# Routing of a mixture of experts rebuilt: transposes and logits inside the last projection, bf16 ranks, three blocks looked up

## The chip, the cores and the metric

The kernel runs on one core of a Trainium2 chip. The metric is the device time of one execution in microseconds (us); lower is better.

## The reference

One decoder block over 512 tokens of 1024 features. A token mixer (short gated convolution and dilated windowed attention, merged by sigmoid gates, then the projection `w_out`) is added to x; then comes the mixture of experts:

```python
h = rms_norm(x, norm2_g)
logits = h @ w_router + b_router                     # 512 x 32
top_vals, top_idx = lax.top_k(logits, 4)
gates = softmax(top_vals)
# each (token, expert) pair gets a place; an expert's places are padded to blocks of 128
# for each block, with its expert e:
gu = xb @ w_gate_up[e] + b_gate_up[e]                # 128 x 2048
act = (clip(up, -7, 7) + 1) * (min(gate, 7) * sigmoid(1.702 * min(gate, 7)))
y = act @ w_down[e] + b_down[e]
out[token] += y * gate_of_the_pair
```

## The kernel before

The engines run programs of their own, tied together by semaphores: PE (matmul), ACT, DVE, POOL, and SP, which issues loads. Large products split each fp32 operand into a high and a low part and take three matmuls (`three`, lines 574 to 576); ACT makes the high part of a weight chunk, DVE the low one (`split`, `split_expert`, lines 865, 987, 1085, 1236). A weight chunk is 1 MB; six buffers take them in, and one is asked for again when DVE is through with it.

**The front** is a fixed list of steps (`STEPS`). Its last four chunks are the projection (`wo`), in units of half the contraction: unit `UF - 1` is the last. Each chunk covers 256 columns, and DVE adds its four blocks of 128 tokens to `x2` (line 1153), while ACT squares and sums them (line 915).

**The routing** then runs as one chain. PE turns `x2` (32 transposes, line 712); ACT and DVE copy the eight results with the gain of the norm; PE makes 32 x 512 logits in eight matmuls (line 721); ACT copies them and PE turns them back. DVE divides by the norm and adds the bias (line 1265), finds maxima and indices (1269, 1270), makes one-hot rows (1273) and their sum (1279). PE sums ranks (729, 733) and counts. For the first two experts' blocks DVE marks which token has which rank (1326), PE multiplies that by token numbers (742), and DVE writes the indices (1338); POOL gathers the rows of block 0 (1473) out of `expert_inputs`, a copy of the normed rows in DRAM which DVE made (1259) and SP stored. PE turns them (754), ACT and DVE split them (1009, 1358), and the expert blocks begin. DVE's first weight split, `split_expert(0, 0)`, stands between the normed rows and line 1265.

**All other blocks** are looked up in a table. DVE works out a place for each of the 16 x 128 pairs, POOL writes them as 16 indirect DMAs (line 1487), reads the table back (1491), stores `x2` as the initial output in five DMAs of 512 KB (1551, 1552), and from then on copies one column per block (1527) and gathers by it (1473). So the first block that hangs on the table is block 2.

**A block** is 16 steps of gate and up (first a bias matmul, line 778), eight of down. The rows of the next block are turned after the second and fourth of the down steps; in block 0, which has no down step, at the end. There the down biases of all experts are also added to `x2`: PE makes each half in eight matmuls (808), DVE adds it in two operations (1397), and block 1 waits for all four:

```python
pe.wait_ge(x2_biased, 2)
down_bias(1)
pe.wait_ge(x2_biased, 4)
```

## Time and profile before

| | |
|---|---|
| Time, three runs | 1715.55 us median (1714.28 to 1716.5) |
| The profiled execution | 1712.57 us, span 1710.7 |
| Busy: PE, DVE, ACT, POOL | 1652.5, 1351.3, 1095.7, 318.4 us |
| Chain that ended last | PE 91%, DVE, POOL and DMA 2% each |
| Mean granted clock of PE | 0.987 |

The span runs from the first to the last instruction. The busy time of PE is modelled, and pipelined matmuls overlap, so the distance from one start to the next tells more than a duration. In a row, the bracket at the end gives how long the engine was idle before it and what ended that.

### The profile page before, as it was taken

How to read it: one execution, taken by the hardware profiler on the slowest of the kernel's cores; microseconds unless marked ns; L12 is line 12 of the kernel's file. 1: busy time of each engine (PE TensorE's matmuls, PEld its weight loads, DVE VectorE, ACT ScalarE, POOL GpSimd, SP SyncE). 2: the span in 40 equal slices, each digit the busy share in tenths (PEclk: the TensorE clock that was granted, in tenths of full speed). 3: DMA queues.
4: the chain of work that ended last, by engine and by line, in shares of the span. 5: the costliest groups of instructions: out<-in, count | busy, mean ns of one | idle time of the engine just before them, and what ended most of it. 6: DMA issues, size and time to landing. Idle time of an engine off the chain costs nothing.

```text
span 1710.7 us, 23870 instructions
## 1 busy us (share of the span) xinstructions
PE 1652.5 (97%) x7974; PEld 1349.4 (79%) x7974; DVE 1351.3 (79%) x1091; ACT 1095.7 (64%) x989; POOL 318.4 (19%) x174
## 2 busy tenths in 40 slices
PE   7999999999997899999999999999999999999995
PEld 5788777888885678888888888888888888888884
DVE  3874555543537989899998999989999899998994
ACT  4324333422344567787777877778777787777873
POOL 0000000510002741221112221132111221113210
PEclk9999999999997999999999999999999999999998
DMA  8222222332436899999999999999999999999993
GB/s 267 79 75 74 74 75 75 93 102 95 143 144 210 296 368 378 367 374 377 383 378 369 366 381 384 376 365 373 383 377 378 366 371 384 382 376 365 376 384 95
DMA packets 211683, 482.34 MB, mean 282 GB/s; under 512 B 12539, under 2 KB 55075, under 8 KB 195123
## 3 DMA queue, kind: packets, MB, share of 16 engines
q1 hardware_dynamic: 201024, 453.99, 70.6%
q0 software_dynamic: 10624, 27.87, 7.9%
q8 instruction: 24, 0.39, 0.1%
q14 instruction: 11, 0.09, 0.0%
HBM read 469.05 MB, written 21.67 MB: 287 GB/s over the span
## 4 chain that ended last, share of the span: by engine, by line
PE 91%; DVE 2%; POOL 2%; DMA 2%; issue 2%; ACT 1%; SPq 0%; POOLq 0%; ACTq 0%; DVEq 0%
PE ps L574 28%; PE ps L576 27%; PE ps L575 27%; PE ps L754 2%; PE ps L760 2%; PE ps L778 2%; POOL slot_records L1487 1%; DMA r<-expert_inputs,uix 1%; PE ps L688 1%; PE ps L677 1%; PE ps L649 1%; PE ps L668 0%; PE ps L721 0%; PE ps L594 0%; ACT work L967 0%
## 5 line engine op out<-in xcount | busy, mean ns | idle before, releaser
L1236 DVE TENSOR_TENSOR zT<-raw,zT 128x2048 fp32r<-128x2048 f32 x96 | 220.0, 2293 | 57.4 <-ACT zT L987 54.6
L1236 DVE TENSOR_TENSOR w_lo<-more_raw,w_hi 128x2048 fp32r<-128x2048 f32 x96 | 217.3, 2290 | 17.7 <-ACT w_hi L987 17.7
L1236 DVE TENSOR_TENSOR zT<-more_raw,zT 128x2048 fp32r<-128x2048 f32 x96 | 219.8, 2290 | 0.0
L1236 DVE TENSOR_TENSOR w_lo<-raw,w_hi 128x2048 fp32r<-128x2048 f32 x96 | 217.1, 2289 | 0.9 <-ACT w_hi L987 0.9
L574 PE MATMUL ps<-w_hi,xT 128*128 128x512 f32 x512 | 216.6, 423 | 0.0
L574 PE MATMUL ps<-zT,xT 128*128 128x512 f32 x512 | 202.4, 395 | 0.0
L576 PE MATMUL ps<-w_hi,xT 128*128 128x512 f32 x512 | 200.7, 392 | 0.0
L575 PE MATMUL ps<-w_lo,xT 128*128 128x512 f32 x512 | 200.7, 392 | 0.0
L987 ACT ACTIVATE zT<-more_raw 128x2048 fp32r<-128x2048 f32 x96 | 183.5, 1911 | 25.6 <-PE ps L576 25.6
L576 PE MATMUL ps<-zT,xT 128*128 128x512 f32 x512 | 199.5, 390 | 0.0
L575 PE MATMUL ps<-zT,xT 128*128 128x512 f32 x512 | 199.3, 389 | 0.0
L987 ACT ACTIVATE w_hi<-raw 128x2048 fp32r<-128x2048 f32 x96 | 183.4, 1910 | 21.3 <-PE ps L576 21.3
L1540 POOL DMA_INDIRECT out<-r,uix x32 | 51.3, 1603 | 714.3 <-ACT r L1036 707.9
L987 ACT ACTIVATE zT<-raw 128x2048 fp32r<-128x2048 f32 x96 | 183.3, 1911 | 0.0
L1085 DVE TENSOR_TENSOR w_lo<-raw,w_hi 128x1024 fp32r<-128x1024 f32 x76 | 101.6, 1349 | 102.5 <-ACT w_hi L865 102.4
L987 ACT ACTIVATE w_hi<-more_raw 128x2048 fp32r<-128x2048 f32 x96 | 180.0, 1909 | 0.0
L574 PE MATMUL ps<-hT,w_hi 128*128 128x512 f32 x416 | 167.3, 402 | 0.0
L575 PE MATMUL ps<-hT,w_hi 128*128 128x512 f32 x416 | 162.4, 390 | 0.0
L576 PE MATMUL ps<-hT,w_lo 128*128 128x512 f32 x416 | 162.0, 389 | 0.0
L865 ACT ACTIVATE w_hi<-raw 128x1024 fp32r<-128x1024 f32 x76 | 79.8, 1056 | 72.3 <-PE ps L576 70.8
L574 PEld LDWEIGHTS ps<-w_hi,xT 128*128 128x128 f32 x512 | 97.5, 190 | 25.2 <-issue 0.6
L576 PEld LDWEIGHTS ps<-w_hi,xT 128*128 128x128 f32 x512 | 96.8, 189 | 21.3
(240 smaller groups left out, 3356.9 us busy)
## 6 DMA issues: line engine op xcount, KB each, us to landing
more_raw<-in_w_gate_up SPq DMA_DIRECT2D x129, 1024.0 KB, 7.4
raw<-in_w_gate_up SPq DMA_DIRECT2D x127, 1024.0 KB, 7.0
raw<-in_w_down SPq DMA_DIRECT2D x65, 1024.0 KB, 8.0
more_raw<-in_w_down SPq DMA_DIRECT2D x63, 1024.0 KB, 7.2
raw<-in_w_in SPq DMA_DIRECT2D x29, 1024.0 KB, 5.2
r<-in_x SPq DMA_DIRECT2D x8, 512.0 KB, 7.1
raw<-in_w_branch_conv SPq DMA_DIRECT2D x4, 1024.0 KB, 4.7
raw<-in_w_out SPq DMA_DIRECT2D x4, 1024.0 KB, 4.7
```

The lines of the kernel that those rows point to most:

```text
L574: pe.matmul(dst, a_hi, b_hi, start=start, stop=False)
L575: pe.matmul(dst, a_hi, b_lo, start=False, stop=False)
L576: return pe.matmul(dst, a_lo, b_hi, start=False, stop=stop)
L649: pe.matmul(ps[:, EVENTS[ev][2], :], cst[:, C_BLK:C_BLK + P], yv[:, j % 2, :], start=True, stop=True).then_inc(done, 1)
L754: last = pe.transpose(ps[:, bk_T + half, P * k:P * k + P], xs[:, 4 * half + k::KD], ident)
L760: last = pe.transpose(ps[:, bk_T + half, P * k:P * k + P], act[:, half, k::4], ident)
L778: pe.matmul(ps[:, base + s, :], sel[:, bass.ds(g, 1), :], bpart[:, D * s + 512 * half:D * s + 512 * half + 512], start=True, stop=False)
L865: nc.scalar.activation(packed(w_hi, n), raw_unit(n, (n // 2) % RAW), ACT.Copy).then_inc(split_hi, 1)
L987: nc.scalar.activation(expert_pair(0, c), chunk, ACT.Copy).then_inc(split_hi, 2)
L1085: nc.vector.tensor_tensor(packed(w_lo, n), raw_unit(n, (n // 2) % RAW), packed(w_hi, n).bitcast(F32), ALU.subtract).then_inc(split_lo, 1)
L1236: nc.vector.tensor_tensor(expert_pair(1, c), chunk, expert_pair(0, c).bitcast(F32), ALU.subtract).then_inc(split_lo, 2)
L1540: nc.gpsimd.indirect_dma_start(out=out, out_offset=bass.IndirectOffsetOnAxis(ap=uix[:, 1:2], axis=0), in_=ysb, in_offset=None, compute_op= ...
```

## The change

- The gain is multiplied in on DVE behind each eviction of the projection, into `h2`. PE turns `h2` instead of `x2`: 16 transposes ahead of the last unit, 8 in its middle, the last 8 behind it. The copies to `h2T` are spread over ACT and DVE (`turn_copy`).
- The logits are made per block of 128 tokens, each in a column group of 32 of its own: four matmuls of 128 columns for each k. Four k are done inside the last unit. They are copied once as 128 x 128 and turned by one transpose.
- The norm's factor is applied to `h2` in place, two blocks on DVE, two on ACT; SP waits for each block by itself.
- DVE's routing works on all four blocks at once, with fewer waits between operations; the sum of one-hot rows is two additions instead of a reduction. Masks, triangle, ones, one-hot rows and token numbers are bf16 (a token number in two parts).
- Three blocks are looked up early: block 0's index first and alone, then 1 and 2. `split_expert(0, 0)` moves behind them. POOL gathers block 2's rows by `gather(4)`, behind the stores but without the table.
- `add_down_bias(1)` comes before `clamp_up(0, 1)`, and PE waits for three of the four additions.

The diff, cut to its core (removed lines of the routing can be seen above; the context is shortened):

```diff
 UPE = 2 * CPE
+GBANK = (0, 1, 2, 3, 0, 1, 3, 0)
 PAIRS = HPG // 2 * NB
...
         load_expert(0, c, 0, first=True)
-    sp.wait_ge(h2_ok, NB)
     for b in range(NB):
+        sp.wait_ge(h2_d if b < 2 else h2_a, b % 2 + 1)
         sp.dma_start(h2_v[:, b, :], h2[:, b, :]).then_inc(h2_out, 16)
...
             src = hT if name == "v" else zT
-            for b in range(NB):
+            for b in rows:
                 ev = EV[(name, 4 * i + b)]
...
                                  wh[:, k, :], wl[:, k, :], kk == 0, kk == KD - 1)
+                if n == UF - 1 and b < NB - 1:
+                    last.then_inc(last_rows, 1)
             return last
...
     for kind, n in STEPS:
-        if kind == "unit":
...
+    def turn_gained(k, rows):
+        pe.wait_ge(gained_ok, NB * (k // 2) + rows[-1] + 1)
+        for b in rows:
+            last = pe.transpose(ps[:, 4 + GBANK[k], P * b:P * b + P], h2[:, b, P * k:P * k + P], ident)
+        return last
+    def logits(k):
+        pe.wait_ge(h2T_d if k % 2 else h2T_a, k // 2 + 1)
         for b in range(NB):
...
+            last = pe.matmul(ps[NE * b:NE * b + NE, 6, 0:P], wr_sb[:, k, :], h2T[:, k, P * b:P * b + P],
+                             start=(k == 0), stop=(k == KD - 1))
+        return last
+    pe.wait_ge(freed["dve"], FREED[EV[("wo", 3 * NB - 1)]][1])
+    for k in range(4):
+        turn_gained(k, range(NB)).then_inc(h2T_pe, 1)
+    unit(UF - 1, rows=(0, 1))
+    pe.wait_ge(h2T_a, 1)
+    pe.wait_ge(h2T_d, 1)
+    for k in (4, 5):
+        turn_gained(k, range(NB)).then_inc(h2T_pe, 1)
     pe.wait_ge(wr_in, 32)
...
+    pe.wait_ge(h2T_a, 2)
+    for k in range(4):
+        logits(k)
+    unit(UF - 1, rows=(2, 3)).then_inc(used, 1)
+    for k in (4, 5):
+        logits(k)
+    for k in (6, 7):
+        turn_gained(k, range(3))
+    for k in (6, 7):
+        turn_gained(k, (3,)).then_inc(h2T_pe, 1)
+    logits(6)
+    logits(7).then_inc(logitsT_pe, 1)
     pe.wait_ge(logitsT_ok, 1)
...
+    pe.transpose(ps[:, 1, 0:P], lgT, ident).then_inc(logit_rows_pe, 1)
+    pe.wait_ge(const_h, 3)
     pe.wait_ge(chosen_ok, 1)
...
+    pe.matmul(ps[:, 1, 0:P], tri_h, mskh.rearrange("p b e -> p (b e)"), start=True, stop=False)
     for c in range(NB - 1):
...
+        last = pe.matmul(ps[:, 1, NE * (c + 1):P].rearrange("p (b e) -> p b e", b=later), ones_h,
+                         mskh[:, c:c + 1, :].to_broadcast([P, later, NE]), start=False, stop=(c == NB - 2))
     last.then_inc(ranks_pe, 1)
...
+        last = pe.matmul(ps[0:NE, 2, 0:1], mskh[:, b, :], ones_h[:, 0:1], start=(b == 0), stop=(b == NB - 1))
     last.then_inc(ranks_pe, 1)
...
+    def early_rows(e):
         pe.wait_ge(hot_ok, e + 1)
...
+            last = pe.matmul(ps[:, bk_T, 2 * e:2 * e + 2], hot[:, e, b, :], tok_h[:, b, :],
                              start=(b == 0), stop=(b == NB - 1))
...
+        return last
+    early_rows(0).then_inc(turned_pe, 1)
+    pe.wait_ge(turned_read, 1)
+    for e in range(1, EARLY):
+        last = early_rows(e)
+    last.then_inc(early_pe, 1)
     pe.wait_ge(blocks_ok, 1)
...
         last.then_inc(turned_pe, 1)
+    pe.wait_ge(early_ok, 1)
     pe.wait_ge(xs_in, 16)
...
     down_bias(1)
-    pe.wait_ge(x2_biased, 4)
+    pe.wait_ge(x2_biased, 3)
     with pe.Fori(1, nblk) as g:
...
         nc.scalar.activation(packed(w_hi, n), raw_unit(n, (n // 2) % RAW), ACT.Copy).then_inc(split_hi, 1)
+    def turn_copy(k):
+        sc.wait_ge(h2T_pe, k + 1)
+        nc.scalar.activation(h2T[:, k, :], ps[:, 4 + GBANK[k], :], ACT.Copy).then_inc(h2T_a, 1)
     sc.wait_ge(eps_ok, 1)
...
                         sc.wait_ge(merged_lo, KD)
+                        sc.wait_ge(logits_ok, PAIRS)
+                    if i == 3 and b == 0:
+                        turn_copy(0)
+                        turn_copy(2)
+                    if i == 3 and b == 2:
+                        turn_copy(4)
                     sc.wait_ge(freed["dve"], FREED[EV[("wo", NB * i + b)]][1])
...
                         sc.wait_ge(ssq, NB + NB * i + b)
-                    nc.scalar.activation(work[:, 0:256], x2[:, b, 256 * i:256 * i + 256], ACT.Square,
+                    nc.scalar.activation(squares, x2[:, b, 256 * i:256 * i + 256], ACT.Square,
                                          accum_out=stat[:, 32 + NB * b + i:33 + NB * b + i]).then_inc(ssq, 1)
...
                          bias=stat[:, 31:32]).then_inc(rstd_s, 1)
-    for k in range(0, KD, 2):
-        sc.wait_ge(h2T_pe, k + 1)
-        nc.scalar.activation(h2T[:, k, :], ps[:, k, :], ACT.Copy,
-                             scale=small[:, 34 + k:35 + k]).then_inc(h2T_a, 1)
+    turn_copy(6)
+    def scale_rows(b):
+        nc.scalar.activation(h2[:, b, :], h2[:, b, :], ACT.Copy, scale=stat[:, 16 + b:17 + b]).then_inc(h2_a, 1)
+    sc.wait_ge(rstd2_ok, 1)
+    sc.wait_ge(h2T_pe, KD)
+    scale_rows(2)
+    sc.wait_ge(logitsT_pe, 1)
+    sc.wait_ge(bias_parts_ok, 1)
+    nc.scalar.activation(lgT, ps[:, 6, 0:P], ACT.Copy).then_inc(logitsT_ok, 1)
+    scale_rows(3)
     for c in range(3):
         split_expert(0, c)
-    sc.wait_ge(logitsT_pe, 1)
-    sc.wait_ge(bias_parts_ok, 1)
-    nc.scalar.activation(lgT, ps[0:NE, 0, :], ACT.Copy).then_inc(logitsT_ok, 1)
     sc.wait_ge(top4_ok, 1)
...
                                        ALU.subtract).then_inc(freed["dve"], 1)
+    def turn_copy(k):
+        ve.wait_ge(h2T_pe, k + 1)
+        nc.vector.tensor_copy(h2T[:, k, :], ps[:, 4 + GBANK[k], :]).then_inc(h2T_d, 1)
     def convolve(m, t):
...
                 continue
+            if name == "wo" and i == 0:
+                ve.wait_ge(scores_pe, PAIRS)
+                nc.vector.tensor_copy(tri_h, cst[:, C_TRI:C_TRI + P]).then_inc(const_h, 1)
+                nc.vector.tensor_copy(ones_h, ones).then_inc(const_h, 1)
+                nc.vector.tensor_copy(mconst[:, 2 * P:2 * P + 2 * NB],
+                                      cst[:, C_TOK:C_TOK + 2 * NB]).then_inc(const_h, 1)
             if name in ("v", "wo"):
...
                     ev = EV[(name, NB * i + b)]
-                    ve.wait_ge(used, n + 1)
+                    if n == UF - 1 and b == 0:
+                        turn_copy(1)
+                        turn_copy(3)
+                    if n == UF - 1 and b == 2:
+                        turn_copy(5)
+                    if n == UF - 1 and b < NB - 1:
+                        ve.wait_ge(last_rows, b + 1)
+                    else:
+                        ve.wait_ge(used, n + 1)
                     src = ps[:, EVENTS[ev][2], 0:256]
...
                         nc.vector.tensor_tensor(dst, src, dst, ALU.add).then_inc(freed["dve"], 1)
+                        ve.wait_ge(freed["dve"], FREED[ev][1])
+                        if i == 0 and b == 0:
+                            ve.wait_ge(g2_in, 16)
+                        nc.vector.tensor_tensor(h2[:, b, 256 * i:256 * i + 256], dst,
+                                                g2b[:, 256 * i:256 * i + 256], ALU.mult).then_inc(gained_ok, 1)
                 continue
...
+    turn_copy(7)
     ve.wait_ge(rstd_s, 2)
...
     ve.wait_ge(rstd2_ok, 1)
+    ve.wait_ge(h2T_pe, KD)
+    for b in range(2):
+        nc.vector.tensor_scalar(h2[:, b, :], h2[:, b, :], stat[:, 16 + b:17 + b], None,
+                                ALU.mult).then_inc(h2_d, 1)
+    ve.wait_ge(logit_rows_pe, 1)
+    link(nc.vector.tensor_tensor(lgt, ps[:, 1, 0:P].rearrange("p (b e) -> p b e", b=NB),
+                                 stat[:, 16:20].unsqueeze(2).to_broadcast([P, NB, NE]), ALU.mult))
+    link(nc.vector.tensor_tensor(lgt, lgt, br_sb.unsqueeze(1).to_broadcast([P, NB, NE]), ALU.add))
     for b in range(NB):
...
+        last = nc.vector.max(top8[:, b, :], lgt[:, b, :])
     link(last)
...
+        last = nc.vector.max_index(idx8[:, b, :], top8[:, b, :], lgt[:, b, :])
+    link(last)
+    link(nc.vector.tensor_scalar(idxf, idx8[:, :, 0:TOPK], 1.0, None, ALU.add))
+    link(nc.vector.tensor_tensor(oh, idxf.rearrange("p b k -> p (b k)").unsqueeze(2).to_broadcast([P, NREC, NE]),
+                                 cst[:, C_IOTA:C_IOTA + NE].unsqueeze(1).to_broadcast([P, NREC, NE]),
+                                 ALU.is_equal))
+    link(nc.vector.tensor_tensor(msk2, ohk[:, :, 0:2], ohk[:, :, 2:4], ALU.add))
+    nc.vector.tensor_tensor(mskh, msk2[:, :, 0], msk2[:, :, 1], ALU.add).then_inc(chosen_ok, 1)
     nc.vector.tensor_tensor(gate, top8[:, :, 0:TOPK], top8[:, :, 0:1].to_broadcast([P, NB, TOPK]),
...
+    link(nc.vector.scalar_tensor_tensor(sg1, ps[:, 1, 0:P].rearrange("p (b e) -> p b e", b=NB), 1.0, mskh,
                                         ALU.add, ALU.mult))
...
+    def find(e):
         nc.vector.tensor_tensor(hot[:, e], cst[:, C_IOTA:C_IOTA + P].unsqueeze(1).to_broadcast([P, NB, P]),
...
                                 ALU.is_equal).then_inc(hot_ok, 1)
+    find(0)
     ve.wait_ge(ranks_pe, 2)
...
     link(nc.vector.tensor_scalar(nbk[:, 1:2], ps[0:NE, 2, 0:1], 2 * P + 0.5, None, ALU.is_gt))
+    ve.wait_ge(turned_pe, 1)
+    ve.wait_ge(ix_set, 1)
+    nc.vector.tensor_copy(stat[:, 26:27], ps[:, bk_T, 0:1]).then_inc(early_hi, 1)
+    ve.wait_ge(early_hi, 1)
+    nc.vector.scalar_tensor_tensor(uix[:, 0:1], stat[:, 26:27], float(OUT_OF_RANGE), ps[:, bk_T, 1:2],
+                                   ALU.add, ALU.add).then_inc(turned_read, 1)
+    for e in range(1, EARLY):
+        find(e)
     link(nc.vector.tensor_scalar(nbk[:, 2:3], ps[0:NE, 2, 0:1], 3 * P + 0.5, None, ALU.is_gt))
...
+    ve.wait_ge(early_pe, 1)
+    nc.vector.tensor_copy(stat[:, 27:29], ps[:, bk_T, 2:2 * EARLY:2]).then_inc(early_hi, 1)
+    ve.wait_ge(early_hi, 2)
+    nc.vector.scalar_tensor_tensor(uix[:, 3:5], stat[:, 27:29], float(OUT_OF_RANGE),
+                                   ps[:, bk_T, 3:2 * EARLY:2], ALU.add, ALU.add).then_inc(early_ok, 1)
+    split_expert(0, 0)
     for b in range(NB):
...
     turned(0, ROWS1, xTh[:, 4:8, :], xTl[:, 4:8, :], bk_T + 1)
+    add_down_bias(1)
     clamp_up(0, 1)
     activate(0, 1)
-    add_down_bias(1)
     split_expert(1, 1)
...
     gp.wait_ge(turned_pe, FIRST_ROWS)
+    gp.wait_ge(early_ok, 1)
     gather(3)
...
     gp.dma_start(out[S:S + P, :], x2[:, 0, :]).then_inc(out_set, 16)
+    gp.wait_ge(turned_pe, tile(1, BEGIN))
+    gather(4)
     gp.wait_ge(slots_in, 16)
-    gather_next(1)
     over_experts()
...
```

## Rows read from the trace of the kernel before

**Rows 1.** Windows: width, busy PE PEld DVE ACT POOL, PEclk, DMA share, GB/s.

```profile
518.00:520.00 2.00, 0.00 (x0) 0.00 (x0) 1.93 (x7) 0.86 (x2) 0.00 (x0) 0.56 0.86 234
...
800.00:1600.00 800.00, 800.00 (x3685) 654.91 (x3684) 744.14 (x495) 636.53 (x495) 173.76 (x90) 1.00 1.03 376
```

**Rows 2.** Timeline of PE: start, us, line, form, count [idle before <-releaser].

```profile
264.15 1.09 PE L688 MATMUL ps<-r 128*64 128x128 f32 x16
...
501.29 0.28 PE L575 MATMUL ps<-w_lo,zT 128*128 128x256 f32 x1
...
501.41 0.28 PE L576 MATMUL ps<-w_hi,zT 128*128 128x256 f32 x1
...
503.20 3.71 PE L712 MATMUL ps<-cst,r 128*128 128x128 f32 x32 [1.51 <-DVE r L1153]
...
506.85 7.05 PE L721 MATMUL ps<-work,r 128*32 128x512 f32 x16
...
520.25 0.79 PE L729 MATMUL ps<-r,cst 128*128 128x128 f32 x2 [5.24 <-DVE r L1279]
...
523.27 3.58 PE L742 MATMUL ps<-cst,work 128*128 128x1 f32 x16 [0.59 <-DVE work L1326]
...
535.74 1.04 PE L778 MATMUL ps<-r 96*128 96x512 bf16 x2 [1.42 <-DVE xT L1358]
...
568.80 1.03 PE L778 MATMUL ps<-r 96*128 96x512 bf16 x2 [4.71 <-DVE r L1397]
...
601.01 1.12 PE L754 MATMUL ps<-cst,r 128*128 128x128 f32 x4 [2.97 <-DMA r<-expert_inputs,uix]
...
612.96 0.61 PE L778 MATMUL ps<-r 96*128 96x512 bf16 x2
```

**Rows 3.** Timeline of DVE, same columns.

```profile
501.73 1.42 DVE L1153 TENSOR_TENSOR r<-ps,r 128x256 f32<-128x256 f32 x4 [10.10 <-PE ps L576]
...
515.05 0.72 DVE L1265 SCALAR_TENSOR_TENSOR r<-ps,stat,r 128x32 f32<-128x32 f32 x4 [0.35 <-PE ps L725]
...
517.91 0.17 DVE L1271 TENSOR_SCALAR r<-r 128x16 f32<-128x16 uint32 x1
...
519.14 1.05 DVE L1279 TENSOR_REDUCE r<-r 128x128 f32<-128x512 f32 x1
...
522.52 1.29 DVE L1326 TENSOR_TENSOR work<-cst,r 128x512 f32<-128x512 f32 x2
...
528.66 2.29 DVE L1236 TENSOR_TENSOR w_lo<-more_raw,w_hi 128x2048 fp32r<-128x2048 f32 x1
...
534.14 0.69 DVE L1358 TENSOR_TENSOR xT<-ps,xT 128x512 fp32r<-128x512 f32 x1 [2.73 <-ACT xT L1009]
...
566.00 2.35 DVE L1397 TENSOR_TENSOR r<-r,ps 128x1024 f32<-128x1024 f32 x2
```

**Rows 4.** Timeline of POOL, and its records as a group (busy, mean ns | idle before).

```profile
527.93 1.26 POOL L1473 DMA_INDIRECT r<-expert_inputs,uix  x1 [6.75 <-DVE uix L1338]
...
545.37 1.01 POOL L1487 DMA_INDIRECT slot_records<-rec,record_at  x1 [9.75 <-issue]
...
585.12 1.92 POOL L1527 COPY uix<-slots 128x1 uint32<-128x1 uint32 x1
...
587.87 2.90 POOL L1473 DMA_INDIRECT r<-expert_inputs,uix  x1 [0.83 <-POOL uix L1527]
...
L1487 POOL DMA_INDIRECT slot_records<-rec,record_at x16 | 24.9, 1558 | 14.3 <-issue 14.3
```

**Rows 5.** DMA issues in 584.58:584.7 and 587.5:588.5: count, KB each, us to landing.

```profile
out<-r POOLq DMA_DIRECT2D x2, 512.0 KB, 13.7
...
r<-expert_inputs,uix POOLq DMA_INDIRECT x1, 13.1
```

**Rows 6.** Groups by form: busy us, mean ns of one | idle before.

```profile
L1273 DVE TENSOR_TENSOR r<-r,cst 128x128 f32<-128x128 f32 x4 | 0.9, 287 | 0.0
...
L865 ACT ACTIVATE w_hi<-raw 128x1024 fp32r<-128x1024 f32 x76 | 79.8, 1056 | 72.3 <-PE ps L576 70.8 <-DMA raw<-in_w_in 1.6
```

More of the change, by code:

```diff
@@ L595, in _, with unit @@
                 last.then_inc(done, 1)
-            def unit(n, tiles=(0, 1)):
+            def unit(n, tiles=(0, 1), rows=range(NB)):
                 name, i = CHUNKS[n // 2]
@@ L693, in _ @@
             for kind, n in STEPS:
-                if kind == "unit":
+                if kind == "unit" and n < UF - 1:
                     unit(n, (1,) if ("half", n) in STEPS else (0, 1)).then_inc(used, 1)
@@ L705, in _ @@
                     values(n)
-            pe.wait_ge(freed["dve"], FREED[EV[("wo", 4 * NB - 1)]][1])
-            for k in range(KD):
-                for b in range(NB):
-                    last = pe.transpose(ps[:, k, P * b:P * b + P], x2[:, b, P * k:P * k + P], ident)
-                last.then_inc(h2T_pe, 1)
-            pe.wait_ge(wr_in, 32)
-            for k in range(KD):
-                if k == 0:
-                    pe.wait_ge(h2T_a, 1)
-                    pe.wait_ge(h2T_d, 1)
-                else:
-                    pe.wait_ge(h2T_d if k % 2 else h2T_a, k // 2 + 1)
-                last = pe.matmul(ps[0:NE, 0, :], wr_sb[:, k, :], h2T[:, k, :], start=(k == 0), stop=(k == KD - 1))
@@ L723, in _ @@
+            for k in (4, 5):
[6 more added lines that the diff above has]
+            logits(7).then_inc(logitsT_pe, 1)
             pe.wait_ge(logitsT_ok, 1)
-            for b in range(NB):
-                last = pe.transpose(ps[:, 1, NE * b:NE * b + NE], lgT[:, P * b:P * b + P], ident[0:NE, 0:NE])
-            last.then_inc(logit_rows_pe, 1)
+            pe.transpose(ps[:, 1, 0:P], lgT, ident).then_inc(logit_rows_pe, 1)
@@ L728, in _ @@
+            pe.wait_ge(const_h, 3)
             pe.wait_ge(chosen_ok, 1)
-            pe.matmul(ps[:, 1, 0:P], cst[:, C_TRI:C_TRI + P], msk.rearrange("p b e -> p (b e)"),
-                      start=True, stop=False)
+            pe.matmul(ps[:, 1, 0:P], tri_h, mskh.rearrange("p b e -> p (b e)"), start=True, stop=False)
             for c in range(NB - 1):
                 later = NB - 1 - c
-                last = pe.matmul(ps[:, 1, NE * (c + 1):P].rearrange("p (b e) -> p b e", b=later), ones,
-                                 msk[:, c:c + 1, :].to_broadcast([P, later, NE]), start=False, stop=(c == NB - 2))
+                last = pe.matmul(ps[:, 1, NE * (c + 1):P].rearrange("p (b e) -> p b e", b=later), ones_h,
+                                 mskh[:, c:c + 1, :].to_broadcast([P, later, NE]), start=False, stop=(c == NB - 2))
@@ L735, in _ @@
             last.then_inc(ranks_pe, 1)
             for b in range(NB):
-                last = pe.matmul(ps[0:NE, 2, 0:1], msk[:, b, :], ones[:, 0:1], start=(b == 0), stop=(b == NB - 1))
+                last = pe.matmul(ps[0:NE, 2, 0:1], mskh[:, b, :], ones_h[:, 0:1], start=(b == 0), stop=(b == NB - 1))
             last.then_inc(ranks_pe, 1)
-            for e in range(2):
+            def early_rows(e):
                 pe.wait_ge(hot_ok, e + 1)
                 for b in range(NB):
-                    last = pe.matmul(ps[:, bk_T, e:e + 1], hot[:, e, b, :], cst[:, C_TOK + b:C_TOK + b + 1],
+                    last = pe.matmul(ps[:, bk_T, 2 * e:2 * e + 2], hot[:, e, b, :], tok_h[:, b, :],
@@ L1256, in _ @@
-            ve.wait_ge(g2_in, 16)
             ve.wait_ge(rstd2_ok, 1)
-            for b in range(NB):
-                nc.vector.scalar_tensor_tensor(h2[:, b, :], x2[:, b, :], stat[:, 16 + b:17 + b], g2b,
-                                               ALU.mult, ALU.mult).then_inc(h2_ok, 1)
-            split_expert(0, 0)
-            ve.wait_ge(logit_rows_pe, 1)
-            for b in range(NB):
-                last = nc.vector.scalar_tensor_tensor(lgt[:, b, :], ps[:, 1, NE * b:NE * b + NE],
-                                                      stat[:, 16 + b:17 + b], br_sb, ALU.mult, ALU.add)
+            ve.wait_ge(h2T_pe, KD)
```

55 lines of the change are left out of this document (20 added, 35 removed).

## Prediction

> **What bounds the kernel now.** I first read the time by stretches. From 800 to 1600 us the matmul engine (PE) is busy all the time at the full clock [rows 1]: the expert blocks run at PE's pace, and what is gained ahead of them reaches the end one for one, as long as weights keep coming. So only the passage from the last projection matmul to block 2 matters. I then walked along it, engine by engine, in the timelines.
>
> PE finishes the projection, and DVE starts the last four evictions at 501.73. Then come, each waiting for the one before, 32 transposes, the logits (7.05), four small transposes, DVE's routing from 515.05 to 520.19 (519.14 + 1.05), the rank sums, the one-hot rows and their eight small products (3.58), the gather of block 0's rows and block 0 at 535.74 [rows 2, 3]. Block 1 starts at 568.80 after 4.71 us in which PE waited for the down-bias additions [rows 2, 3].
>
> There is a second chain, and it decides. POOL writes the 16 records from 545.37 on, loads the slots, sends out five 512 KB blocks, copies the column and gathers block 2's rows at 587.87 [rows 4]. This gather takes 13.1 us [rows 5]. PE has waited 2.97 for it when it goes on at 601.01, and block 2 starts at 612.96 [rows 2].
>
> **Up to the logits.** Sixteen transposes (columns 0 to 511) move ahead of the last unit, eight more into its middle; the work is the same, 3.71/32 = 0.116 each [rows 2]. What goes is the wait for four evictions plus squares and copies behind them. The price of 32 logit matmuls of 128 columns in four column groups isn't in the trace. Bounds: at the old pace of 7.05 us for 8 x 512 columns, 0.88 for each k, nothing is saved; wholly side by side, 0.22. The nearest row is the attention's product with values, two column groups of 64: 16 instructions, so 8 matmuls of 128 columns, took 1.09 where the pace of the logits (7.05/32 = 0.22 for 128 columns) gives 1.76 [rows 2]. They overlap, and an instruction comes about every 0.06. Eight instructions for a k then make 0.46, which I take.
>
> Timeline, on the clock of the trace. The last unit is 48 matmuls, 0.12 from one to the next (501.29 to 501.41), so 5.76, and its predecessor ends at 501.53 - 5.76 = 495.77 [rows 2]. Then 16 transposes 1.84, half of the unit 2.88, 8 transposes 0.93, four k of logits 1.84, the other half 2.88: the last row block is issued at 506.1. DVE evicts it from 506.3 (one of the four in 1.42, alone 0.42) and multiplies by the gain (the same size, 0.42 and a semaphore): 507.2 [rows 3]. Meanwhile PE does k 4 and 5 and six transposes. The last two transposes end at 508.1, the two copies out of PSUM (0.7 like any 128x512 operation of DVE) at 508.8, k 6 and 7 at 509.9. On ACT the scaling of 1024 columns (1.06 [rows 6]) stands ahead of the copy of the logits: 509.1 to 510.15, the copy some 0.3, one transpose: DVE starts the routing at 510.8 instead of 515.05. Gain 4.25; bounds 0.9 (0.88 for each k, three groups of which lie on the path) and 5.1 (0.22).
>
> At one place a rule speaks against this. The Trainium skill, "TensorEngine Tiling (Array Packing)", section Key Properties, says that a change of the tiling mode drains the array; the change has three more such switches than before. By it each switch would add a stop to PE's order where the trace's rows let me price none; no run here shows it for 32-column groups.
>
> **Up to the gather.** DVE's 5.14 us of routing fall: the four maxima and searches (515.8 to 517.91, 2.1) lose most of their eight waits, about 1.5 [rows 3]; four comparisons of 128 columns (0.287 alone [rows 6]) become one of 512 (0.7, no gain but one start); the reduction of 1.05 becomes additions of 256 and 128 columns, 0.42 + 0.29. With the two first operations (0.6) and the cast (0.2) about 3.8: gain 1.35. The rank sums run in fp32, two instructions each, from 520.25 until DVE reads them at 522.2, one operation of 0.3 ahead of the 522.52 of the one-hot rows [rows 2, 3]; in bf16 it is one instruction each, 0.22 at the pace of the sixteen in 3.58, so 0.8 to 0.9: gain 1.15 (bounds 0, if the two passes had overlapped, and 1.6). The first one-hot operation costs what it did. The products of 3.58 become four instructions instead of 16, at most 0.9 and, without fp32 loads, I take 0.55; DVE's reading becomes two operations instead of one (+0.2). From PE's 523.27 to POOL's 527.93 [rows 2, 4] were 4.66, I take 1.85: gain 2.8. Sum: 4.25 + 1.35 + 1.15 + 2.8 = 9.55, gather at 518.4. The rows must be in DRAM by then: ACT scales the last block until 511.6, its store takes 4 to 6, POOL's clearing 1: 517 to 518.5, just hidden, so a gain beyond this would stop here.
>
> **Block 0 starts with less.** Two more lookups (0.65 each), three small operations, the second index pair with its wait (0.7) and above all the weight split of 2.29, which before lay in PE's logits, now stand in DVE's queue behind the first index [rows 3]. Before, DVE had 2.73 us to spare in the gather's shadow, as the row of 534.14 shows. The new work is about 4.5. So DVE becomes the last one by 1.8, and block 0 starts 9.55 - 1.8 = **7.8** earlier, at 527.9. The sixth weight chunk is asked for only after this split, but it is used 16 us into the block: hidden.
>
> **Block 1.** The first half of the second bias addition (one of the two in 2.35) now comes before three operations of 0.7 and its other half: PE's 4.71 fall by about 3.0 [rows 2, 3]. The wait that is left, 1.7, is like the 1.51 after which the logits ran at full speed; 4.71 was followed by matmuls at 1.2 GHz (two bf16 ones of 512 columns in 1.03), as in 518 to 520, where the granted clock shows 0.56 after PE had stood since 515 [rows 1, 2]. So the clock's loss of 1.9 goes too (nine matmuls 0.2 longer). These 4.9 us bring PE only earlier to the gather of block 2. The second split of block 1 is late by 1 to 2 us now, inside the same shadow.
>
> **The gather of block 2.** Records, slots and stores follow DVE's places, so they move by 7.8. The copy (1.92) and its wait (0.83) ahead of the gather go, so it is issued 10.3 earlier. But the last two of the five stores needed 13.7 us [rows 5] and so landed near 598, the gather 3 us behind at 601: it is the queue behind which it stands, not the issue, that sets the landing. Only the stores' shift counts, 7.8, and about 1 more, since PE stands from about 586 and its weight buffers fill: less traffic beside the queue. PE goes on 8.8 earlier, from 601.0 to 592.2, again in the slow clock, and the 11.95 to block 2 stay. From there nothing differs. **Sum: 8.8.** Bounds of this term: 7.8 (nothing but the shift) and 10.3 (issue decides).
>
> The profiled execution took 1712.57 (span 1710.7, 1.9 around it); minus 8.8 is 1703.8. The median of the runs is 3.0 above that execution, so **1706.8**.
>
> **The rivals.**
> - The landing follows the issue, or the front gains its upper bounds: 10.3 to 12, about 1704.5. For it: the gather was 3 us behind the stores, so some of its time was its own. Chance 0.14.
> - The column groups don't overlap in fp32: 0.88 for each k, 3.4 more on the path, gain 5.3, time 1710.2. For it: no 32-column case in the trace; against it: the 64-column row. Chance 0.12.
> - The change does hardly anything: block 0 starts earlier, but DVE's queue, now with the split in front, and POOL's records eat it; gain under 3.4. That takes another 5 us in DVE's queue. Chance 0.07.
> - Slower: the records. They took 1.56 on average, 0.3 between, 0.97 to 2.88 each [rows 4], and short ones are those that meet a gap of DVE. With DVE packed tightly, all at the long form of 2.88 + 0.3, sixteen take 51 instead of 29.5: 21 later, minus 8.8, slower by 12, about 1728. It decides from a mean of 2.4 a record on. Against it: DVE was already busy nine tenths there. Chance 0.05. The Trainium skill, "SBUF — State Buffer", section "SBUF: two separate sides", gives a reason: GpSimd is blocked by whichever DVE operation holds the pair; by that page two-input DVE operations hinder only its reads, which would make this rival less likely.
>
> **The numbers.** My forecast, 7 to 10.3 less: 0.62. The range must hold 8 in 10: from 1703 (a gain of 12.5) to 1711.3 (4.3), which takes in the fp32 rival. A change within 0.2%, 3.4 us, is about what a measurement of this kernel can't tell from none. Faster: 0.62 + 0.14 + 0.12 = 0.88; within 0.2%: 0.07; slower 0.05.
>
> **What would show it.** The logits' 32 matmuls at 0.4 to 0.5 for four; routing on DVE starting near 510.8; the first gather near 518.4; block 0 near 528, released by DVE; no slow clock in block 1; PE waiting 5 to 7 for block 2's rows until about 592; block 2 at 604. Wrong it would be through logits at 0.9 for each k, a store of the rows that ends after 518, records of over 2 us, or a gather of block 2 that PE doesn't wait for.

## The result and the profile after

The changed kernel took 1700.57 us (median of four runs, 1699.39 to 1701.14) where the kernel before took 1714.91 beside it (four runs, 1712.37 to 1716.5): ratio 0.9917, 95% interval 0.99 to 0.9934. In a second comparison it was 1700.6 against 1713.12, ratio 0.9929 (0.9916 to 0.9943). Faster, by 12.5 to 14.3 us; I had forecast 8.8 less and 1706.8, and the time lies below my range. The profiled execution took 1699.39, span 1697.6: 13.2 less than the one of before.

PE's timeline of the changed kernel answers to [rows 2]. Its columns are start, duration, line, operands, and in brackets the idle time before and who ended it. Line 724 is the 32 transposes, 731 the logits, 761 to 768 the ranks, 774 the one-hot products, 792 the turning of gathered rows, 817 the bias matmul that opens a step:

```profile
495.70 1.91 PE L724 MATMUL ps<-cst,r 128*128 128x128 f32 x16
...
500.33 1.04 PE L724 MATMUL ps<-cst,r 128*128 128x128 f32 x8
501.29 1.08 PE L731 MATMUL ps<-work,r 128*32 128x128 f32 x32
502.30 0.39 PE L583 MATMUL ps<-w_hi,zT 128*128 128x256 f32 x1
...
505.36 0.64 PE L731 MATMUL ps<-work,r 128*32 128x128 f32 x16
505.94 1.09 PE L724 MATMUL ps<-cst,r 128*128 128x128 f32 x8
507.61 0.64 PE L731 MATMUL ps<-work,r 128*32 128x128 f32 x16 [0.58 <-ACT work L910]
509.24 0.33 PE L757 MATMUL ps<-cst,r 128*128 128x128 f32 x1 [0.99 <-ACT r L1054]
513.38 0.26 PE L761 MATMUL ps<-r 128*128 128x128 bf16 x1 [3.81 <-DVE r L1349]
...
514.92 0.27 PE L774 MATMUL ps<-r,work 128*128 128x2 bf16 x4 [0.92 <-DVE work L1399]
...
521.25 1.94 PE L792 MATMUL ps<-cst,r 128*128 128x128 f32 x8 [2.47 <-DMA r<-expert_inputs,uix]
525.38 1.03 PE L817 MATMUL ps<-r 96*128 96x512 bf16 x2 [2.19 <-DVE xT L1443]
...
555.48 0.60 PE L817 MATMUL ps<-r 96*128 96x512 bf16 x2 [1.75 <-DVE r L1482]
...
588.54 1.12 PE L792 MATMUL ps<-cst,r 128*128 128x128 f32 x4 [4.40 <-DMA r<-expert_inputs,uix]
...
600.18 0.60 PE L817 MATMUL ps<-r 96*128 96x512 bf16 x2
```

The 32 logit instructions, four k of four column groups in two passes each, take 1.01 (501.29 to 502.30, where the next matmul starts), 0.25 for each k against 0.88 before. Block 0 starts 10.36 earlier (525.38 against 535.74), the rows of block 2 are turned 12.47 earlier (588.54 against 601.01) and block 2 starts 12.78 earlier (600.18 against 612.96).

DVE's timeline answers to [rows 3]:

```profile
509.61 0.29 DVE L1335 TENSOR_TENSOR r<-ps,stat 128x128 f32<-128x128 f32 x1 [0.32 <-PE ps L757]
...
512.95 0.29 DVE L1349 TENSOR_TENSOR r<-r 128x128 bf16<-128x128 f32 x1
...
513.84 0.29 DVE L1355 SCALAR_TENSOR_TENSOR r<-ps,r 128x128 f32<-128x128 f32 x1 [0.52 <-PE ps L764]
...
515.47 0.15 DVE L1411 SCALAR_TENSOR_TENSOR uix<-stat,ps 128x1 uint32<-128x1 f32 x1
...
517.46 2.29 DVE L1316 TENSOR_TENSOR w_lo<-more_raw,w_hi 128x2048 fp32r<-128x2048 f32 x1
...
521.38 2.29 DVE L1316 TENSOR_TENSOR w_lo<-more_raw,w_hi 128x2048 fp32r<-128x2048 f32 x1
...
524.04 1.28 DVE L1443 TENSOR_TENSOR xT<-ps,xT 128x512 fp32r<-128x512 f32 x2
```

Routing starts at 509.61 instead of 515.05. The subtractions of 524.04, which release block 0, have no idle time ahead of them: DVE's own queue is what block 0 now waits for, as forecast.

POOL's timeline answers to [rows 4], and the issues of POOL's queue in a narrow window, with the time to landing, to [rows 5]:

```profile
515.30 0.95 POOL L1554 MEMSET r<- 128x1024 f32 x1 [167.31 <-DMA expert_inputs<-r]
516.54 1.42 POOL L1559 DMA_INDIRECT r<-expert_inputs,uix  x1 [0.29 <-POOL r L1554]
...
568.31 0.60 POOL L1578 DMA_DIRECT2D slots<-slot_records  x1 [4.93 <-DMA slot_records<-rec,record_at]
570.20 2.17 POOL L1638 DMA_DIRECT2D out<-r  x4 [1.29 <-issue]
572.36 0.53 POOL L1639 DMA_DIRECT2D out<-r  x1
573.20 1.09 POOL L1559 DMA_INDIRECT r<-expert_inputs,uix  x1 [0.30 <-issue]
```

```profile
r<-expert_inputs,uix POOLq DMA_INDIRECT x1, 15.3
```

The first gather stands behind POOL's clearing (515.30 + 0.95), which waits for the store of the rows; the index was ready at 515.62, the clearing at 516.25. So a routing that ended earlier would gain nothing more at this place, unless the rows were scaled and stored earlier too. The gather of block 2's rows (the second block above, in which the issue takes 15.3 to land) is issued 14.67 earlier (573.20 against 587.87) and lands 12.4 earlier (573.20 + 15.3 = 588.5, against 587.87 + 13.1 = 601.0).

The granted clock (the column behind the engines' busy times) in three windows answers to [rows 1] and to the slow first matmul at 568.80 in [rows 2]: in block 1's wait of this execution it stays full, after the wait for block 2's rows it is the lower level of 1.2 GHz.

```profile
554.00:556.00 2.00, 0.52 (x3) 0.38 (x4) 2.00 (x2) 0.31 (x1) 1.70 (x2) 1.00 0.96 341
588.00:590.00 2.00, 1.46 (x6) 1.36 (x7) 0.00 (x0) 0.30 (x1) 2.00 (x1) 0.50 1.05 395
592.00:594.00 2.00, 2.00 (x6) 1.57 (x5) 2.00 (x2) 0.10 (x1) 1.92 (x2) 0.54 1.05 389
```

### The profile page after: what moved, and what is told of

Read it like the earlier page. It is cut to its first block, busy times and chain, and to the rows that moved or that the text cites. A ratio compares the mean times of both kernels' runs of the same rounds, so it can differ in the third digit from the quotient of the medians.

```text
span 1697.6 us, 23961 instructions
## 1 busy us (share of the span) xinstructions
PE 1641.4 (97%) x8007; PEld 1343.6 (79%) x8007; DVE 1353.6 (80%) x1108; ACT 1096.3 (65%) x991; POOL 313.8 (18%) x173
## 4 chain that ended last, share of the span: by engine, by line
PE 91%; DVE 3%; POOL 2%; issue 2%; DMA 1%; ACT 1%; SPq 0%; POOLq 0%; ACTq 0%; DVEq 0%
PE ps L583 28%; PE ps L585 27%; PE ps L584 27%; PE ps L798 2%; PE ps L792 2%; PE ps L817 2%; POOL slot_records L1574 1%; DMA r<-expert_inputs,uix 1%; PE ps L699 1%; PE ps L688 1%; PE ps L660 1%; PE ps L679 0%; PE ps L603 0%; DVE w_lo L1316 0%; ACT work L1017 0%
```

## The experiments

My theory after the result: the front's gain reaches block 0, and from there block 2, because POOL's stores and with them the gather follow block 0. Rivals: the gather goes by its issue; the bias order or the clock gave part of the gain; single parts of the front gave nothing. Ratios are to the kernel before on the same chip; the changed kernel's are the two above.

**When the gather is issued.** Block 2's rows looked up late, from the slots, as before:

```
-            gather(4)              # rows looked up from ranks
             gp.wait_ge(slots_in, 16)
+            gather_next(1)         # column copied from slots
             over_experts()
```

> Block 2's rows are gathered by the column of the table again, behind the stores, everything else as changed. Theory Q (the stores on POOL's queue set the landing, 588.5 against the last store's 587.7): the gather is issued some 2.5 us later, at 575.7, but lands no more than 1 to 2 later, so 0 to 2 us slower than the changed kernel. Rival I (the issue sets the landing): 2.5 to 3 slower. Rival P (the forecast's missing 5 us come from the third lookup itself): 5 or more slower.

Measured: 1700.07, ratio 0.9924 (0.991 to 0.9937), as the changed kernel. Its front happened to run 1.2 us earlier (block 0 at 524.21). POOL issued the gather at 576.65, 3.45 later than in the changed kernel, and PE turned the rows at 589.22 after 5.92 of waiting, only 0.68 later. In the changed kernel's second profile (the run `after_again` below) the issue is at 573.70 and the rows are turned at 587.71; against that one the late lookup costs 1.51 of 2.95. So the queue of the five stores swallows half to four fifths of what the early lookup takes off the issue, in kind as the prediction had it, and the median shows nothing of the rest. Now the gather put ahead of them, right behind the last record:

```
+            gather(4)
             gp.wait_ge(slots_out, 16 * NREC)
             (load slots, five stores)
-            gather(4)
```

> The gather of block 2's rows is issued right behind the 16 records (at about 563.4) and ahead of the table's load and the five stores. Theory Q: it lands by 575, PE's wait of 4.4 us at 588.5 and the slow clock behind it (about 2.5 us) go, so 6 to 7 us faster than the changed kernel, and block 2 starts near 593.5. Rival R (block 2 is held by something else right behind, such as weights or the rows of block 3): 0 to 3 faster.

Measured: 1698.11, ratio 0.9912 (0.9897 to 0.9927): 14.6 less than the kernel before, where the changed kernel is 12.5 to 14.3 less. I had expected 6 to 7 more than that; rival R held. Ahead of the stores the gather lands in 9.2 instead of 15.3:

```profile
r<-expert_inputs,uix POOLq DMA_INDIRECT x1, 9.2
```

The rows are there before PE wants them; PE's wait comes some 5 us later in the block and for something else. Five rows of this kernel, from the timelines of PE, ACT, DVE and POOL:

```profile
592.96 0.64 PE L583 MATMUL ps<-zT,oT 128*128 128x512 f32 x1 [3.22 <-DVE zT L1316]
```

```profile
591.87 1.91 ACT L1037 ACTIVATE w_hi<-raw 128x2048 fp32r<-128x2048 f32 x1 [1.91 <-DMA raw<-in_w_gate_up]
```

```profile
586.62 4.08 DVE L1468 SCALAR_TENSOR_TENSOR work<-work 128x512 f32<-128x512 f32 x1
590.62 2.28 DVE L1316 TENSOR_TENSOR zT<-more_raw,zT 128x2048 fp32r<-128x2048 f32 x1
```

```profile
586.54 5.13 POOL L1604 TENSOR_SCALAR r<-r,cst 96x1920 bf16<-96x1920 f32 x1
```

An operation that takes 0.69 elsewhere took 4.08 on DVE, starting 0.08 behind POOL's long one; the weight split behind it (590.62) was late without any idle time of its own, and PE waited 3.22 for it. The load for which ACT waited 1.91 feeds a later chunk: it was late too, but PE did not wait for it here. Block 2 started at 597.40, only 2.8 earlier than in the changed kernel, though the rows no longer cost anything.

**The order of the bias additions.** The old order and wait, alone and with the gather ahead:

```
-            add_down_bias(1)
             clamp_up(0, 1)
             activate(0, 1)
+            add_down_bias(1)
...
-            pe.wait_ge(x2_biased, 3)
+            pe.wait_ge(x2_biased, 4)
```

> The second half of the down bias is added behind the activation again and PE waits for all four additions, everything else as changed. Theory Q: block 1 starts about 3 us later and in the slow clock, 5 us in all, but this lies in front of PE's 4.4 us of wait for block 2's rows (5.3 with what surrounds it), so 0 to 1 slower than the changed kernel, the wait for the rows nearly gone. Rival S (the time follows PE's own chain): 4 to 5 slower.

> Both: the gather ahead of the stores, and the bias additions in the old order. Theory Q: with the wait for the rows gone nothing hides the old order, so it costs 4 to 5 us against the kernel with the gather ahead alone, and comes out 1.5 to 3 faster than the changed kernel. Rival S: the same 4 to 5 as in the kernel without the gather ahead.

Measured: alone 1700.85, ratio 0.9934 (0.9921 to 0.9948); with the gather ahead 1700.65, ratio 0.9927 (0.9914 to 0.9941). The row of PE and two windows of the kernel with the old order alone:

```profile
559.02 1.03 PE L817 MATMUL ps<-r 96*128 96x512 bf16 x2 [5.16 <-DVE r L1482]
```

```profile
556.00:558.00 2.00, 0.00 (x0) 0.00 (x0) 2.00 (x3) 0.00 (x0) 1.70 (x2) 1.00 0.25 34
558.00:560.00 2.00, 0.98 (x3) 0.62 (x4) 2.00 (x2) 1.25 (x3) 1.70 (x2) 0.54 0.02 1
```

The wait grows from 1.75 to 5.16 and the clock falls behind it, which is the old state of [rows 2]. (It also falls in some executions with the short wait, see below.) Block 2 starts at 599.97 all the same, 0.2 from the changed kernel: these us lie in front of block 2's rows and are free. The wait of 4.40 for the rows is gone (PE turns them at 588.47 without idle time), and PE waits 1.91 for a weight split instead: DVE's line 1468 took 2.85 beside POOL's long operation. With the gather ahead the old order is not free: block 2 at 599.78 instead of 597.40, 2.4 us, where I had expected 4 to 5. What is hidden is not gone; it depends on the next wait.

**The logits in one group.** One matmul of 512 columns for each k, a longer copy and four small transposes:

```
-                for b in range(NB):
-                    last = pe.matmul(ps[NE * b:NE * b + NE, 6, 0:P], wr_sb[:, k, :],
-                                     h2T[:, k, P * b:P * b + P], ...)
+                return pe.matmul(ps[0:NE, 6, :], wr_sb[:, k, :], h2T[:, k, :], ...)
```

> The logits are made as one group of 32 output rows and 512 columns for each k, copied as 32 x 512 and turned by four transposes; all else as changed. If the four column groups overlap fully, as the 0.24 us for each k in the changed kernel says, this costs 0.64 for each of eight k, some 5 us, of which k 0 to 3, 4 and 5 and 6 and 7 all delay the last evictions or follow them; with 0.3 for the longer copy and transposes the first gather comes 5 later, and 4.5 to 5.5 us are lost. If part of it hides behind evictions and scaling: 3 to 4. My forecast's size (0.46 for each k) would have made it 3.4.

Measured: 1704.53, ratio 0.9946 (0.9933 to 0.9959). PE:

```profile
501.45 3.62 PE L730 MATMUL ps<-work,r 128*32 128x512 f32 x8
...
508.06 1.90 PE L730 MATMUL ps<-work,r 128*32 128x512 f32 x4
```

Four k now take 3.55 (501.45 to 505.00, where the next matmul starts), 0.89 each, where the groups took 0.25. Block 0 starts at 530.38, 5.0 later than in the changed kernel, and block 2 at 604.90, 4.7 later: what the front gains or loses does reach block 2 nearly one for one.

**The ranks and one-hot rows in fp32.** Same matmuls, masks and constants in fp32. The buffers are changed as below; the three copies on DVE that made the bf16 constants, long before the routing, go with them:

```
-        mskh = tail[:, 1540:1604].bitcast(BF16)...
+        mskh = tail[:, 1540:1668]...
-        hot = work[:, 2560:2560 + EARLY * 256].bitcast(BF16)...
+        hot = work[:, 2560:2560 + EARLY * 512]...
```

> Masks, triangle, ones, one-hot rows and token numbers are fp32 again, the order as changed. Rank sums +1.3, the first product with token numbers +1.4 (eight instructions at 0.22 instead of 0.25 in all), the other two +3 but in DVE's shadow: the first gather 2.7 later, of which about 1 goes into the slack by which DVE is late for block 0 now, if the second lookup does not delay DVE too. So 2 to 3.5 us slower. Rival: the rows' way to DRAM and POOL's clearing, which ended at the same moment as the index, hold the gather anyway: under 1.

Measured: 1705.75, ratio 0.9958 (0.9945 to 0.9972), the dearest part to undo and more than the 2 to 3.5 that I expected. Routing starts at 509.58 as in the changed kernel, but the rank sums reach DVE at 515.21 after 1.92 of waiting (513.84 and 0.52), and the products are:

```profile
516.29 1.87 PE L772 MATMUL ps<-cst,work 128*128 128x2 f32 x8 [0.59 <-DVE work L1393]
519.35 3.54 PE L772 MATMUL ps<-cst,work 128*128 128x2 f32 x16 [1.19 <-DVE work L1393]
```

1.87 for block 0 and 3.54 for the two other blocks, in place of four instructions of 0.27 in all for each. The second, which I had put into DVE's shadow, is the larger cost: DVE waits 2.71 for it, and with it the split that block 0 stands behind. Block 0 at 531.12 (5.7 later), block 2 at 606.80 (6.6 later).

**The weight split ahead of the routing**, where the kernel before had it:

```
             (gain of the last row block) .then_inc(h2_d, 1)
+            split_expert(0, 0)
             ve.wait_ge(logit_rows_pe, 1)
```

> DVE's first weight split stands before the routing again. It needs ACT's high part, which is ready only at 512, so DVE starts the routing at 514.3 instead of 509.6: 4.6 later, less 1.0 by which block 0 is released by DVE's queue now: 3 to 4 us slower. If DVE's queue were not what released block 0: 4.6 slower. If the place of the split did not matter: 0.

Measured: 1703.82, ratio 0.9946 (0.9933 to 0.996). In this order DVE waits for ACT's copy of the weights and goes into the split at

```profile
511.46 2.29 DVE L1316 TENSOR_TENSOR w_lo<-more_raw,w_hi 128x2048 fp32r<-128x2048 f32 x1 [2.83 <-ACT w_hi L1037]
```

and starts the routing at 513.67, 4.1 later. Block 0 gets 0.7 of it back (528.68, 3.3 later), since DVE is then in time for it (1.13 us to spare at the subtraction). Block 2 at 603.27, 3.1 later. In the new front, whose logits leave no shadow for it, putting the split behind the first index is thus worth 3.1 us, where my prediction only counted it as a cost.

**The records' places ahead of two splits**, so that POOL starts earlier:

```
-            split_expert(0, 2)
-            split_expert(0, 3)
             place_records()
             gates()
+            split_expert(0, 2)
+            split_expert(0, 3)
```

> DVE works out the places of the records before the weight splits 2 and 3 of block 0, so POOL starts the records 4.4 us earlier; PE's third weight chunk comes just in time. Theory Q: the whole chain of records, table, stores and gather moves by 4.4, PE's wait of 4.4 for block 2's rows and the slow clock behind it go: 4 to 7 us faster than the changed kernel. Rival: PE starves for the third chunk in block 0 by up to 2 us, which is hidden in front of the rows: still 3 to 5 faster. If records do not set the time: 0.

Measured: 1697.47 (1692.87 to 1698.11), ratio 0.9894 (0.9879 to 0.9909), the best ratio of all, though its interval overlaps those of its neighbours. The first record starts at 530.58, 4.4 earlier, the slots are loaded at 566.21, 2.1 earlier, the rows turned at 586.30 (2.2 earlier) and block 2 starts at 597.14 (3.0 earlier). Half of the head start went into longer records (30.3 from first to last instead of 28.4) and a longer wait for their landing (5.29 instead of 4.93), so block 2 gains 3 and not the 4 to 7 that I expected.

**The two kernels again, and two combinations.**

> The changed kernel once more, without an edit, to see how far its profiled execution and its median move by themselves, and to have it beside the next two on one chip. Theory: the profile after showed 13.2 us less than the profile before, and the medians 14.3; if the chain of records really gained 1.85 us more than block 0, this profile shows the slots loaded at 568.3 again, within 0.5, block 0 at 525.4 and block 2 at 600.2. Rival: the records scatter by themselves; then the slots come at 568 to 571 with block 0 unmoved, and block 2 follows them. Median in either case 1699.5 to 1701.5.

> The kernel before once more, without an edit, for a second profile of its records. Theory: block 0 at 535.7, slots loaded at 580.5 within 0.5, rows of block 2 landed at 601. Rival: the records scatter; the slots come between 578.5 and 582, and the wait for block 2's rows moves with them, which would make 1 to 2 us of the difference between the two kernels a matter of the one execution.

Measured: the changed kernel's profile repeats (block 0 at 525.73, slots at 568.82, block 2 at 599.71, span 1697.1). The kernel before does not; PE, then DVE and POOL:

```profile
598.28 0.71 PE L754 MATMUL ps<-cst,r 128*128 128x128 f32 x4
...
607.65 0.50 PE L574 MATMUL ps<-zT,oT 128*128 128x512 f32 x1 [2.67 <-DVE zT L1236]
```

```profile
601.32 4.08 DVE L1383 SCALAR_TENSOR_TENSOR work<-work 128x512 f32<-128x512 f32 x1
```

```profile
576.86 0.60 POOL L1491 DMA_DIRECT2D slots<-slot_records  x1 [4.03 <-DMA slot_records<-rec,record_at]
...
601.23 5.13 POOL L1515 TENSOR_SCALAR r<-r,cst 96x1920 bf16<-96x1920 f32 x1
```

The slots came 3.7 earlier than in the profile that I predicted from (580.53), and the rows without a wait (584.38 + 13.9 = 598.3). The block did not start 3 us earlier for that, but 1.0 (611.96): POOL's long operation met DVE's, the split was late, PE waited 2.67 for it, and the clock fell behind the wait (0.71 in 608 to 610, 0.50 in 610 to 612). So the kernel before had two bounds within 3 us of each other, the rows and the weight split held up by POOL, and an execution may end on either.

> Two edits together: the records' places and the gates ahead of two weight splits on DVE, and the gather of block 2's rows right behind the records, ahead of the slots and the five stores. Alone they gave 16.2 us less than the kernel before for the first and 14.6 for the second, where the changed kernel gave 14.3. Theory of one bound behind another: with the rows there early the stores' queue no longer counts, and what is left are the weights, which land late beside the stores, and DVE's splits; the stores are 2 us earlier here, so the weights' late time is too and meets other chunks: block 2 at 596.5 to 597.5, median 16 to 17.5 less than before, not the sum of the two (20). Rival: the gains add, block 2 at 594.5, median 1694.5 to 1696.

> The gather of block 2's rows right behind the records, and one more weight split of block 0 moved behind the eviction of its rows. If DVE's queue is what releases block 0 (its subtractions stood without idle time from 524.04 on, with the transposes on PE done at 523.2), block 0 starts 0.8 to 1.2 us earlier, at 524.3, and the weights of block 0 are asked for no later than they are used. Theory: block 0's own start gives nothing behind block 2 unless the records move too; they are placed behind the same splits, so they stay, and the median is that of the gather moved alone, 14 to 15 less than before. Rival: the start of block 0 reaches the end, 15.5 to 16 less.

Measured: places and gather both ahead 1697.58 (1694.6 to 1698.08), ratio 0.9911 (0.9895 to 0.9926); not the sum of the two gains. Its profile has block 2 at 595.37, and DVE's line 1468 takes 2.14 while POOL's line 1604 runs: the same second bound, though PE waits only 1.23 there. With the split behind the subtractions, 1700.04, ratio 0.9922 (0.9909 to 0.9936): block 0 gets its rows turned and subtracted 0.8 sooner behind the gather (3.36 between lines 792 and 817 instead of 4.13), but PE waits 0.85 and 0.68 for that split inside block 0, and the places, which stand behind it on DVE, let the first record start at 537.02 instead of 535.00. PE then meets the second bound again (line 1468 takes 4.09, PE waits 3.04), and block 2 is at 600.23. Neither of my two expectations held there.

## Why the prediction was wrong

The direction, the chain of causes and the last wait were right; the sum was too small. Of the 6.2 us between 1706.8 and 1700.6, 4.0 lie ahead of block 2 (forecast 604.16, measured 600.18):

- **Up to the logits: the step that failed first.** I took 0.46 for each k, measured 0.25, near the lower bound of 0.22. I had turned the 64-column row of [rows 2] into a pace for each instruction (0.06) and kept that pace for four groups. In the changed kernel an instruction comes every 0.03 (1.01/32). The row behind it, which I did not show, gives the start-to-start time:

```profile
265.07 0.61 PE L688 MATMUL ps<-work,r 128*64 128x128 f32 x8
```

  Eight matmuls of 128 columns took 0.92 (264.15 to 265.07) where one after another would take 1.76: two groups already ran side by side, by a factor of 1.9. Carried over as a factor, that gives four groups 0.23 for each k. On the path stood the four k ahead of the last row block (1.01 instead of 1.84) and k 4 and 5 ahead of the last transposes (0.58 instead of 0.92). These 1.17 are nearly the whole miss: routing started at 509.6 instead of 510.8, gain 5.44 against 4.25, and my upper bound of 5.1 was too low as well. The kernel with one group, its longer copy and its four transposes included, loses 5.0 at block 0. The Trainium skill, "TensorEngine Tiling (Array Packing)", section Key Properties, lets a change of tiling mode drain the array. Here four k took 1.01 and two k 0.58 (505.36 to 505.94), each with the switch in and out. By my estimate from these two, 0.215 goes to each k and 0.15 to the two switches, so a drain, if there was one, cost under 0.1.
- **Up to the gather**: routing to the cast mask gained 1.5 (forecast 1.35), the rank sums 1.4 (1.15), the rest up to the gather 3.0 (2.8). Together 0.6 missed. Gather at 516.54, forecast 518.4. The store of the rows, which I thought "just hidden" at 517 to 518.5, came by 515.30; with the clearing behind it, it ends 0.6 after the index and is now what the gather waits for.
- **DVE late for block 0**: right in kind; 8.84 between gather and block 0 instead of 7.81, so 1.0 and not 1.8. These three together make block 0 start 10.36 earlier instead of 7.8: 2.56 of the 4.0.
- **Block 1**: PE's wait fell from 4.71 to 1.75 (forecast 1.7). That the slow clock would go with it held in this execution and not in every one. In the changed kernel's second profile the wait is 1.85, and the clock falls behind it:

```profile
556.00:558.00 2.00, 2.00 (x6) 1.51 (x7) 1.91 (x4) 1.31 (x3) 1.52 (x2) 0.56 0.12 33
```

  It also falls with the gather ahead and with the places first (0.50 in the same window, waits of 1.75 and 2.02). All of this is hidden, as the old order showed (block 2 within 0.2 us).
- **The gather of block 2**: that the stores' queue and not the issue sets the landing was right (issue 14.67 earlier, landing 12.4; a late lookup cost 0.7 of its 3.45, or 1.5 of 2.95 against the second profile). The size was off: landing moved 2.1 more than block 0, where I had 1.0. Of this, 1.85 is that the slots came 12.2 earlier. The second profile of before has them 3.7 earlier than the first, with block 0 only 0.9 earlier. So the scatter of the execution I started from is large enough to give all of it, and I ascribe none of it to the change.
- **From the rows to block 2** 11.64 instead of 11.95, and 0.4 behind block 2.
- **The base.** I added 3.0, the distance of that execution from the median of 1715.55; medians of before in the four comparisons were 1712.68 to 1714.91, and the changed kernel's profile stands 1.2 below its median. The difference, 1.8, is the rest of the miss.

My list of signs held but for sizes and for the clock in block 1: PE waited 4.4 for the rows, until 588.5, not 5 to 7 until 592. The rivals: groups that don't overlap are refuted (0.25 against 0.89); longer records too (28.4 from first to last, 29.5 before). "The landing follows the issue, or the front gains its upper bounds" was half right: the front did, the landing didn't, and its 1704.5 was still too high. The range allowed a gain of 12.5. The profiled pair alone moved by 13.2, so it was too narrow even without the base: all terms but those hidden missed to the same side, the first beyond its bound. On top of that I never asked how far the base itself moves.

Open: why three of nine runs of the kernels with the places first lie 3 to 5 us below the others (1692.87, 1693.72 and 1694.6). The one of them that was profiled (1694.6) has block 2 at 595.37 and the clock kept up behind the last wait, which gives 1.8 and 1.7 against the profile of places first; for the other two no trace says it.

## What to carry to other kernels

Undo each part alone: three parts of this front were worth 5.0, 5.7 and 3.3 at block 0, more than the 10.4 of the whole change. Each is priced with the others in place, so the prices don't add up. The fourth, the bias order, moved block 2 by 0.2, and its interval overlaps those of the changed kernel. The early transposes and DVE's routing on all blocks at once were not undone alone; their worth is read from the trace only. And an order that looked like a cost (the split behind the index) was a gain, because what stood first in DVE's queue waited for another engine. Before summing savings in front of a wait, look for the second bound right behind it, from a second execution if there is one: here it stood 1 to 3 us away, and it is what moving the gather ran into. When two bounds move together with the front, its gain passes nearly one for one.

## What the runs showed of the hardware

- Four fp32 matmuls of 32 output rows in four column groups run side by side: 0.25 for each k of 4 x 128 columns, where one matmul of 512 columns takes 0.89.
- DVE's operation with two inputs from SBUF (line 1468, in the kernel before 1383) took 4.08 or 4.09 instead of 0.69 when it started 0.07 to 0.09 behind POOL's 5.13 one, in three kernels (gather ahead, before again, split later). Started later beside it, it took 2.85, 2.48, 2.14, 1.65 and 1.57 in five others, and in all eight it ended 0.96 or 0.97 ahead of the end of POOL's record, whenever it had begun. In the kernel with the gather ahead and the old bias order the turn fell the other way. Here line 1468 kept its 0.69, POOL's operation took 5.68, and DVE's next one, a weight split that takes 2.29 elsewhere, took 5.63:

```profile
589.04 0.69 DVE L1468 SCALAR_TENSOR_TENSOR work<-work 128x512 f32<-128x512 f32 x1
589.65 5.63 DVE L1316 TENSOR_TENSOR zT<-more_raw,zT 128x2048 fp32r<-128x2048 f32 x1
```

  Operations that read PSUM were not held up: in the changed kernel lines 1473 and 1463 ran at 590.33 and 590.94, in the midst of POOL's operation of 587.78 to 592.91, in 0.69 and 0.68. The Trainium skill, "SBUF — State Buffer", section "SBUF: two separate sides", says that the shared port pair is an exclusive lock that whoever starts first holds for its whole instruction, for DVE operations with two SBUF inputs only against a GpSimd operation that reads SBUF. The trace agrees on which operations are held up and that one blocks the other; that DVE's ends 0.97 ahead of POOL's record it does not explain, and spans on POOL are rough. No run moved POOL's operation alone; the common end is the evidence.
- A wait of the same length may or may not drop the clock, in block 1 (above) and near the end. There PE's wait of 2.0 us in two executions of the kernel before, left the granted clock at full in the one and dropped it in the other; windows of the first and of the second execution:

```profile
1685.00:1690.00 5.00, 5.00 (x24) 4.12 (x23) 4.42 (x2) 2.29 (x2) 1.12 (x1) 1.00 0.69 104
```

```profile
1685.00:1690.00 5.00, 5.00 (x18) 3.97 (x17) 4.21 (x2) 1.41 (x1) 0.26 (x1) 0.76 0.70 105
```

  From block 2 to the end it was 1097.7 in the first and 1099.6 in the second. Of the twelve profiles after the change, the six where the clock stayed up show 1097.3 to 1097.7, the six where it fell 1098.9 to 1099.2 (both old bias orders, one group, the split ahead of the routing, the gather ahead, the places first). That is 1.9 us between two executions of one kernel, as much as some of the edits here are worth, and the reason why the parts are compared at block 0 and block 2 above.
- The front itself scatters: the last of PE's logit transposes (line 757) started between 508.09 and 509.70 in the nine profiles of eight kernels whose code up to there is the same on all engines.
